# One decoder block on one core: places freed by the products themselves, the first head routed alone, the second tile's attention pairs at slots 8 to 24

## The chip, the core and the metric

The kernel runs on one core of one Trainium2 chip. A core has a matrix engine (PE, TensorE), a vector engine (DVE, VectorE), a scalar engine (ACT, ScalarE), GpSimd (POOL) and a queue engine (SP, SyncE), which run apart from each other and meet at semaphores; 16 DMA engines move data between device memory and the on-chip memory. The metric is the device time of one execution in microseconds (us). The kernel before takes 834.14 us, the median of three runs (832.98 to 834.54).

## The reference, cut to what matters

256 tokens of width 1024 go through one block: a modulation computed from a vector `c`, attention of 16 heads (8 with one causal block, 8 dilated, which on 256 tokens are masks over the same scores), an output projection, a layer norm, and a feed-forward part that picks experts for each token.

```python
mod = silu(c) @ w_ada + b_ada                       # 1024 x 6144
sh1, sc1, g1, sh2, sc2, g2 = split(mod, 6)
h = x * (1 + sc1) + sh1
proj = h @ w_in                                     # 1024 x 3072: q, k, v of both groups
y = rms_norm(attention(proj)) @ w_out
x = layer_norm(ALPHA * x + (1 + g1) * y)
h2 = x * (1 + sc2) + sh2
q = h2 @ w_q                                        # 8 heads of 128
s1, s2 = q[:, :, :64] @ keys0.T, q[:, :, 64:] @ keys1.T      # 128 scores each
e, g = top 16 of the 16 x 16 sums of the top 16 of s1 and of s2, and their softmax
a = gelu(h2 . u[e]) * g                             # 8 x 16 experts for each token
out = layer_norm(ALPHA * x + (1 + g2) * sum(a * v[e]))
```

Each of the 256 tokens reads 128 experts, each a row of 2048 floats (u and v, 8 KB): 268 MB in all.

## The kernel before, in words

**Tiles.** Tokens are two tiles of 128. The gather part has 256 *slots*, 128 to a tile and 16 to a head. A slot is one expert for each of 128 tokens: one indirect DMA by POOL (L1065) brings 1 MB into one *place* of `ring`. DVE takes the dot product of h2 with the row's first half (`dot`, L814); ACT makes gelu, weight and a diagonal matrix of weights (`weigh`, L647 to L660); PE multiplies that matrix by the row's second half and adds it up in two banks (`slot`, L465). Three slots of each 16 between 16 and 111 (`BY_DVE`) are added by DVE instead (`add_slot`, L825 to L828). A gather may start when the slot before it in its place is done.

**Places.** The ring has eight places of 8 KB per partition. Before the gathers they hold the chunks of the weights, so they come free late: 4 and 5 after product `v 1 1`, 6 and 7 after `q 0 1`, 0 and 1 after `v 0 1`, 2 and 3 after the second tile's output products `wo 1 g 0`. Gathers 0 to 35 (`WIDE_FROM`) go round six places (`NARROW`), the later ones round all eight. That a pair is free is told by ACT: a step `free` in its stream waits for the product and counts up `ring_free` (L748), on which POOL waits.

**Order.** One list, `PLAN`, names all steps, and every engine walks through it and does its own part of each step, so the list sets the order on every engine. `gather_steps(i)` gives the steps at slot i: its dot, pieces of the routing of a later head (`piece`, 12 to a head, L845 to L888), what `BESIDE` lists for i, and the products of slot i - 2. `BESIDE` holds the second tile's attention: `S` (scores), `Tr` (transposes), `PV` (values) for pairs of units, then `wo`, `xa`, `ln1a`, `ln1b` (output product, residual, norm) and the queries `q` and scores `s` of the other heads.

**The steps named below.** `wsum c` is the product of silu(c) with column chunk c of `w_ada` on DVE: 8 instructions of 128x512 (L924 or L928, then L937). For chunk 2, terms 3, 6 and 7 are made by PE (`modk`, L521). `modp` and `modc` are column sums on PE (L475) that give shift and scale; `modrow` and `madd` spread the other chunks over the partitions. `qkz`, `qkh`, `qk` are the query and key products (L525, L490), split by halves of the weights. The bias row of the attention is made by PE (`bias`, L533) in bank 0 and read by DVE (L895). A 1 is added to three rows of `mod` by POOL (L1055, L1056). Chunk 11 is loaded as four *patches* into parts of other tiles, since no place is free. `q 0 0` makes the queries of heads 0 and 1 for the first tile, `s 0 0 z` their scores; the routing of head 0 follows, and its end lets the first gather start.

**Banks.** The steps that fill a bank take banks 0 to 5 in turn; two steps (`LATE`) have banks 6 and 7.

## Time and profile before

| | before |
|---|---|
| median of three runs | 834.14 us (832.98 to 834.54) |
| profiled execution, its time and its span | 833.26 us, 831.4 us |
| PE, DVE, ACT, POOL busy | 687.7, 586.9, 340.1, 306.2 us |
| DMA | 323.72 MB, 389 GB/s over the span; 78.2% of the span in the gathers' queue |
| chain that ended last | DMA 52%, PE 29%, DVE 8%, ACT 4% |

The profile is of one execution; its first instruction starts at 0 and its last ends at 831.4 us, so about 1.9 us of that execution's time lie around the span. Busy time is by engine and may overlap. A view of a line, an engine or a stretch gives start and length of instructions, how long the engine was idle before, and what released it; an instruction of PE on 32-bit floats shows as two rows' worth of passes, so 16 products count as x32. The DMA share in a stretch tells how full the 16 DMA engines were, and GB/s what they moved.

### The profile page before, as it was taken

Reading aid. Unit: us, or ns where it says so; the run is one execution under the profiler, and the core shown is the slowest. Engines: PE = TensorE matmul, PEld = TensorE weight load, DVE = VectorE, ACT = ScalarE, POOL = GpSimd, SP = SyncE. Lnnn points to the kernel's source line nnn. Section 1 sums busy time; section 2 is a strip of 40 time slices with the busy share of each in tenths; the row PEclk is TensorE's granted clock in tenths of the full one; section 3 lists DMA queues with packets and bytes.
Section 4 is the critical chain, followed back from the end, with each engine's and each line's share of the span. In section 5 each row is a group of like instructions: output and inputs, shape, how many; then the busy total and the mean of one; then the engine's idle time right before and its main releaser. Section 6 shows DMA issues by size and latency. Waiting matters only on the chain.

```text
span 831.4 us, 7233 instructions
## 1 busy us (share of the span) xinstructions
PE 687.7 (83%) x2000; PEld 330.8 (40%) x2000; DVE 586.9 (71%) x1296; ACT 340.1 (41%) x988; POOL 306.2 (37%) x263
## 2 busy tenths in 40 slices
PE   6999999799998878786979877777778687878874
PEld 3887745545434444442423323222223232222221
DVE  6645886689689767787777777767576757675545
ACT  0012142376636343434454536344443434343333
POOL 5000000234356535554535444543443434434320
PEclk9999999999999998998898999999999999999998
DMA  9999992399999999999999999999999999999991
GB/s 353 401 419 419 376 388 82 149 401 392 375 394 396 421 421 421 421 421 422 421 422 421 421 421 421 423 421 420 421 422 421 422 422 423 420 421 423 420 422 75
DMA packets 48043, 323.72 MB, mean 389 GB/s; under 512 B 5698, under 2 KB 8066, under 8 KB 9346
## 3 DMA queue, kind: packets, MB, share of 16 engines
q0 software_dynamic: 36864, 268.45, 78.2%
q1 hardware_dynamic: 10258, 54.55, 16.5%
q10 hardware_dynamic: 882, 0.27, 0.1%
q8 instruction: 16, 0.26, 0.1%
...
HBM read 322.18 MB, written 1.07 MB: 389 GB/s over the span
## 4 chain that ended last, share of the span: by engine, by line
DMA 52%; PE 29%; DVE 8%; ACT 4%; issue 4%; POOL 2%; SPq 0%; DVEq 0%; ACTq 0%
DMA ring<-in_experts,e_all 50%; PE bank L465 14%; PE bank L490 6%; PE bank L456 4%; DVE ring L814 3%; DVE acc L937 2%; POOL ring L1065 2%; ACT diag L660 1%; DMA lnw<-in_w 1%; PE bank L560 1%; PE bank L579 1%; ACT weight L651 1%; DMA ring<-in_w 1%; ACT gel L647 1%; PE bank L521 1%
## 5 line engine op out<-in xcount | busy, mean ns | idle before, releaser
L465 PE MATMUL bank<-ring,diag 128*128 128x512 f32 x952 | 472.3, 632 | 113.4 <-ACT diag L660 112.8
L1065 POOL DMA_INDIRECT ring<-in_experts,e_all x256 | 293.8, 1148 | 490.7 <-PE bank L465 293.4
L465 PEld LDWEIGHTS bank<-ring,diag 128*128 128x128 f32 x952 | 172.8, 196 | 391.5 <-ACT diag L660 236.8
L814 DVE CUSTOM_DVE_ANT_0 ring<-ring,T_h 128x1024 f32<-128x1024 f32 x128 | 156.8, 1226 | 113.0 <-DMA ring<-in_experts,e_all 113.0
L814 DVE CUSTOM_DVE_ANT_0 ring<-ring,h 128x1024 f32<-128x1024 f32 x128 | 156.7, 1224 | 74.0 <-DMA ring<-in_experts,e_all 72.6
L647 ACT ACTIVATE gel<-pre 128x1 f32<-128x1 f32 x256 | 51.9, 203 | 332.4 <-DVE pre L814 331.5
L660 ACT ACTIVATE diag<-consts,weight 128x128 f32<-128x128 f32 x238 | 95.5, 401 | 7.8
L651 ACT ACTIVATE weight<-gel,g_all 128x1 f32<-128x1 f32 x256 | 75.4, 295 | 9.3
L937 DVE SCALAR_TENSOR_TENSOR acc<-ring,cact,acc 128x512 f32<-128x512 f32 x60 | 49.0, 817 | 2.8
L456 PE MATMUL bank<-ring,hT_yT 128*128 128x512 f32 x80 | 35.5, 594 | 0.0
L490 PE MATMUL bank<-hT_yT,lnw 128*128 128x256 f32 x128 | 30.8, 402 | 1.1 <-DVE hT_yT L907 1.1
L668 ACT COPY QT_h2T<-bank 128x512 f32<-128x512 f32 x6 | 3.5, 580 | 61.0 <-PE bank L490 61.0
L490 PEld LDWEIGHTS bank<-hT_yT,lnw 128*128 128x128 f32 x128 | 25.9, 204 | 5.5 <-issue 1.6
L647 ACT ACT_TABLE_LOAD x21 | 26.9, 1283 | 0.4
L456 PEld LDWEIGHTS bank<-ring,hT_yT 128*128 128x128 f32 x80 | 15.0, 190 | 18.3 <-issue 18.2
L828 DVE SCALAR_TENSOR_TENSOR hT_yT<-ring,weight,hT_yT 128x1024 f32<-128x1024 f32 x17 | 21.8, 1281 | 0.0
L814 DVE DVE_READ_ACCUMULATOR2_ANT pre<- 128x1 f32 x256 | 21.1, 83 | 0.0
L641 ACT ACT_TABLE_LOAD x15 | 19.2, 1283 | 0.3
L701 ACT ACTIVATE probs<-probs,negmax 128x128 f32<-128x128 f32 (+1 forms) x32 | 14.2, 443 | 11.0 <-DVE negmax L957 11.0
L954 DVE SCALAR_TENSOR_TENSOR probs<-bank,T_h 128x512 f32<-128x512 f32 x12 | 8.2, 682 | 10.1 <-PE bank L560 10.1
L579 PE MATMUL bank<-V_x,probs 128*128 128x64 f32 x96 | 11.7, 274 | 4.2 <-issue 4.2
L579 PEld LDWEIGHTS bank<-V_x,probs 128*128 128x128 f32 x96 | 11.6, 192 | 7.4 <-issue 7.4
...
## 6 DMA issues: line engine op xcount, KB each, us to landing
ring<-in_w SPq DMA_DIRECT2D x28, 1024.0 KB, 12.9
H_s<-in_w SPq DMA_DIRECT2D x7, 1024.0 KB, 13.8
lnw<-in_w SPq DMA_DIRECT2D x6, 1024.0 KB, 15.6
ring<-in_experts,e_all POOLq DMA_INDIRECT x256
...
xT_y<-in_xT SPq DMA_DIRECT2D x1, 1024.0 KB, 13.8
x<-in_x SPq DMA_DIRECT2D x1, 1024.0 KB, 16.9
...
```

What stands on the lines that cost most here:

```text
L456: last = nc.tensor.matmul(dst, lhs(k), rhs(k), start=(k == 0), stop=(k == n - 1))
L465: last = nc.tensor.matmul(tile_sum(t)[n], diag[:, m % DIAGS, :], ring[:, RING_AT[i], D + CH * n:D + CH * n + CH], start=(s == 0), stop=(s ...
L490: last = nc.tensor.matmul(dst[:, T * j:T * j + T], w[:, k, P * (2 * i + j):P * (2 * i + j) + P], hT[:, k, :], start=(k == 0 and c >= 2), s ...
L579: last = nc.tensor.matmul(dst[:, HD * j:HD * j + HD], probT[:, step[1] % 2, at:at + P], V_x1[:, kt, c:c + HD], start=(kt == 0), stop=(kt = ...
L641: nc.scalar.activation(bexp[:], bdiff[:], ACT.Exp, accum_out=bsum[:, 0:1]).then_inc(bexp_ready, 1)
L647: own.then(nc.scalar.activation(gel[:, r:r + 1], pre[:, r:r + 1], ACT.Gelu))
L651: ins = nc.scalar.mul(weight[:, r:r + 1], gel[:, r:r + 1], g_all[:, i:i + 1])
L660: nc.scalar.mul(diag[:, m % DIAGS, :], ident, weight[:, r:r + 1]).then_inc(diag_ready, 1)
L814: nc.vector.tensor_tensor_reduce(ring[:, r, 0:D], ring[:, r, 0:D], h2[i // SLOTS], 1.0, 0.0, ALU.mult, ALU.add, pre[:, i % PAIR:i % PAIR + ...
L828: ins = nc.vector.scalar_tensor_tensor(dve_sum, values, weight[:, r:r + 1], dve_sum, ALU.mult, ALU.add)
L937: ins = nc.vector.scalar_tensor_tensor(part, row, cact[:, k:k + 1], part, ALU.mult, ALU.add)
L1065: nc.gpsimd.indirect_dma_start(ring[:, r, :], None, A["experts"], bass.IndirectOffsetOnAxis(ap=e_all[:, i:i + 1], axis=0)).then_inc(slot_i ...
```

## The change

1. `free` and `ring_free` go. POOL waits itself for the bank of the product that empties a pair of places.
2. Of head 0, queries and scores are made alone (`q1 0`, `s1 0 z`), then those of head 1; `q` starts on half of the transposed tile.
3. `wsum 11` moves on DVE from after `wsum 10` to after `ln1b 0`. Its patches change (one of them in `diag`), and the second output chunk is loaded ahead of them on SP. `wsum 7` goes ahead of `yT 0 0`.
4. POOL's additions of 1 go; ACT adds it as the bias of its copy (`madd`).
5. In the opening, `bias` and `modc 0` get banks 6 and 7, term 6 of chunk 2 goes from PE to DVE, and PE has four more products whose result isn't used (`warm`).
6. The second tile's pairs go from slots 0 to 19 to slots 5 to 24, and what follows them from 20 to 32 to 25 to 45. `WIDE_FROM` goes from 36 to 44. A fourth slot in each 16 is added by DVE.
7. ACT loads the table of gelu after `v 0 1` is issued (`gelu`), and copies `v 0 1` at slot 1.
8. Each residual takes its two halves one after the other, and the last slot of a tile signals its first half (`half_done`).

```diff
-BY_PE = {2: (3, 6, 7)}
+BY_PE = {2: (3, 7)}
-WIDE_FROM = 36
+WIDE_FROM = 44
-       ("v", 1, 1), ("free", 0), ("ln1b", 0), ("hT", 0, 0), ("hT", 0, 1), ("S", 4), ("q", 0, 0),
-       ("s", 0, 0, 0), ("s", 0, 0, 1), ("Tr", 4), ("modrow", 7)]
+     ("v", 1, 1), ("ln1b", 0), ("wsum", 11), ("hT", 0, 0), ("hT", 0, 1), ("S", 4), ("q1", 0), ("s1", 0, 0), ("s1", 0, 1), ("q1", 1), ("Tr", 4), ("modrow", 7)]
-BY_DVE = [i for i in range(16, 112) if i % 16 in (2, 4, 5)]
+BY_DVE = [i for i in range(16, 112) if i % 16 in (2, 4, 5, 12)]
...
+APART = [("bias",), ("modc", 0)] + [("wo", 0, 1, n) for n in range(2)]
...
             load(("ada", 10))
+            filled(sp, ("qk", 3, 1))
+            load(("out", 1))
             summed(sp, 9)
...
-            filled(sp, ("qk", 3, 1))
-            load(("out", 1))
...
+                    if s == SLOTS - 1 and n == 0:
+                        last.then_inc(half_done, 1)
...
+                if kind == "warm":
+                    w = places[W_PLACES[CHUNK[("ada", 0)]]]
+                    arrived(pe, CHUNK[("ada", 0)], 0)
+                    for _ in range(step[1]):
+                        nc.tensor.matmul(bank[STEP_BANKS - 1][:, 0:T], ones[:], w[:, 0, 0:T], start=True, stop=True)
...
+                elif kind == "q1":
+                    h = step[1]
+                    w = query_weights(pe, 0, 0)
...
+                    product(dst[:, 0:P], lambda k: w(k)[:, P * h:P * h + P], tokens).then_inc(full, 1)
+                elif kind == "s1":
+                    h, z = step[1:]
+                    pe.wait_ge(gnsk_in, 32)
+                    settle_bank(pe, ("q1", h))
+                    r = slice(HD * z, HD * z + HD)
+                    nc.tensor.matmul(dst[:, 0:NK], query_T(0, 0)[r, h, :], skT[r, :], start=True, stop=True).then_inc(full, 1)
...
+                        nc.scalar.activation(part, src[:], ACT.Identity, bias=ones[:, 0:1]).then_inc(freed(("modrow", m)), 1)
...
+                elif kind == "s1":
+                    act.wait_ge(patch_read, 1)
+                    evacuate(step, scores[:, 0, step[1], step[2], :], filled(act, step)[:, 0:NK])
...
-                for n in range(2):
-                    dve.wait_ge(*f[n][2])
+                    dve.wait_ge(*taken)
...
-            pool.wait_ge(rows_in, 16)
-            nc.gpsimd.tensor_scalar(mod[0:1, G1, :], mod[0:1, G1, :], 1.0, None, ALU.add)
-            nc.gpsimd.tensor_scalar(mod[0:1, SC2:G2 + 1, :], mod[0:1, SC2:G2 + 1, :], 1.0, None, ALU.add).then_inc(rows_one, 1)
+            empty = {4: [("v", 1, 1)], 6: [("q", 0, 1)], 0: [("v", 0, 1)], 2: [("wo", 1, g, 0) for g in range(2)]}
...
-                    pool.wait_ge(ring_free, 1 + sum(before is None for before in RING_BEFORE[:i]))
+                    for step in empty[r // 2 * 2]:
+                        filled(pool, step)
```

The order on PE at the very start, before; the one-column products of `bank<-cact,ring` are `modk`, those of `bank<-ones,acc` are `modp` and `modc`, and the last row is `qkh`:

```order
L525 MATMUL bank<-acc 128x512 x3
L533 MATMUL bank<-probs,relT 16x384
L525 MATMUL bank<-acc 128x512
L513 MATMUL bank<-acc 128x16
L475 MATMUL bank<-ones,acc 128x1 x4
L521 MATMUL bank<-cact,ring 128x1 x12
L475 MATMUL bank<-ones,acc 128x1 x4
L490 MATMUL bank<-hT_yT,lnw 128x256 x16
```

And now; the rows `bank<-ring,ones` are `warm`:

```order
L535 MATMUL bank<-acc 128x512 x3
L543 MATMUL bank<-probs,relT 16x384
L535 MATMUL bank<-acc 128x512
L519 MATMUL bank<-acc 128x16
L524 MATMUL bank<-ring,ones 128x256 x2
L531 MATMUL bank<-cact,ring 128x1 x4
L480 MATMUL bank<-ones,acc 128x1 x4
L524 MATMUL bank<-ring,ones 128x256
L531 MATMUL bank<-cact,ring 128x1 x4
L524 MATMUL bank<-ring,ones 128x256
L480 MATMUL bank<-ones,acc 128x1 x4
L495 MATMUL bank<-hT_yT,lnw 128x256 x16
```

The bias row and the shift have other banks, four of the twelve `modk` rows are gone, and the column sums of chunk 0 come after the first `modk`.

The order on DVE from the norm of the first tile (its last instruction is `h_0<-h_0,lnst,mod`) to the start of head 0's routing (`MAX`), before; `probs` is pair 4 of the attention:

```order
L797 SCALAR_TENSOR_TENSOR h_0<-x,lnst,mod 128x1024
L802 RECIPROCAL lnst<-lnst 128x1
L808 SCALAR_TENSOR_TENSOR h_0<-h_0,lnst,mod 128x1024
L954 SCALAR_TENSOR_TENSOR probs<-bank,T_h 128x512
L957 TENSOR_REDUCE negmax<-probs 128x2
L845 MAX v<-H_s 128x8 x2
```

And now, where the rows with `cact` are `wsum 11`:

```order
L825 SCALAR_TENSOR_TENSOR h_0<-x,lnst,mod 128x1024
L830 RECIPROCAL lnst<-lnst 128x1
L836 SCALAR_TENSOR_TENSOR h_0<-h_0,lnst,mod 128x1024
L956 SCALAR_TENSOR_TENSOR acc<-H_s,cact,mod 128x512
L967 SCALAR_TENSOR_TENSOR acc<-H_s,cact,acc 128x512 x3
L967 SCALAR_TENSOR_TENSOR acc<-xT_y,cact,acc 128x512 x2
L967 SCALAR_TENSOR_TENSOR acc<-V_x,cact,acc 128x512
L967 SCALAR_TENSOR_TENSOR acc<-diag,cact,acc 128x512
L984 SCALAR_TENSOR_TENSOR probs<-bank,T_h 128x512
L987 TENSOR_REDUCE negmax<-probs 128x2
L873 MAX v<-H_s 128x8 x2
```

Eight instructions stand now ahead of pair 4 and of the routing.

The order on PE from the transposes of the first tile to the product `v 0 1` (`bank<-ring,hT_yT`), before; `bank<-xT_y,ring` are queries, `bank<-skT,acc` their scores:

```order
L599 MATMUL bank<-consts,h_0 128x128 x8
L560 MATMUL bank<-KT_qT,QT_h2T 128x256 x2
L456 MATMUL bank<-xT_y,ring 128x128 x16
L616 MATMUL bank<-skT,acc 128x128 x4
L567 MATMUL bank<-consts,probs 128x128 x4
L550 MATMUL bank<-acc,ones 128x512
L456 MATMUL bank<-xT_y,ring 128x128 x16
L616 MATMUL bank<-skT,acc 128x128 x4
L560 MATMUL bank<-KT_qT,QT_h2T 128x256 x2
L579 MATMUL bank<-V_x,probs 128x64 x4
L456 MATMUL bank<-ring,hT_yT 128x512 x8
```

And now:

```order
L609 MATMUL bank<-consts,h_0 128x128 x8
L570 MATMUL bank<-KT_qT,QT_h2T 128x256 x2
L459 MATMUL bank<-xT_y,ring 128x128 x8
L639 MATMUL bank<-skT,acc 128x128 x2
L459 MATMUL bank<-xT_y,ring 128x128 x8
L577 MATMUL bank<-consts,probs 128x128 x4
L560 MATMUL bank<-acc,ones 128x512
L639 MATMUL bank<-skT,acc 128x128 x2
L459 MATMUL bank<-xT_y,ring 128x128 x16
L646 MATMUL bank<-skT,acc 128x128 x4
L570 MATMUL bank<-KT_qT,QT_h2T 128x256 x2
L589 MATMUL bank<-V_x,probs 128x64 x4
L459 MATMUL bank<-ring,hT_yT 128x512 x8
```

Eight products of queries instead of sixteen stand ahead of the first scores.

## Rows read from the trace of the kernel before

**Rows 1.** the page's second part: GB/s moved by the DMA engines in 40 slices.

```profile
GB/s 353 401 419 419 376 388 82 149 401 392 375 394 396 421 421 421 421 421 422 421 422 421 421 421 421 423 421 420 421 422 421 422 422 423 420 421 423 420 422 75
```

**Rows 2.** windows: busy time and count per engine, granted PE clock, DMA share, GB/s.

```profile
140.00:156.00 16.00, 13.74 (x109) 11.87 (x107) 9.41 (x35) 7.13 (x18) 0.00 (x0) 1.00 0.00 1
156.00:168.00 12.00, 8.85 (x31) 4.77 (x31) 6.17 (x21) 5.23 (x13) 5.85 (x6) 0.98 0.82 319
168.00:200.00 32.00, 29.60 (x101) 15.05 (x100) 28.20 (x78) 23.36 (x60) 11.13 (x10) 0.95 1.00 400
200.00:260.00 60.00, 56.34 (x186) 28.57 (x184) 49.53 (x118) 33.76 (x89) 31.72 (x23) 1.00 0.98 380
360.00:800.00 440.00, 352.66 (x762) 131.49 (x760) 304.59 (x709) 193.18 (x581) 192.59 (x177) 0.97 1.01 421
```

**Rows 3.** timeline: start, length, instruction, count, [idle before]. POOL, then DVE.

```profile
13.99 5.68 POOL L1056 TENSOR_SCALAR mod<-mod 1x2048 f32<-1x2048 f32 x1
...
14.48 4.01 DVE L937 SCALAR_TENSOR_TENSOR acc<-ring,cact,acc 128x512 f32<-128x512 f32 x1
```

**Rows 4.** timeline of PE, 18 to 52 us.

```profile
18.14 5.26 PE L521 MATMUL bank<-cact,ring 128*128 128x1 f32 x24
...
26.17 9.56 PE L490 MATMUL bank<-hT_yT,lnw 128*128 128x256 f32 x32 [1.07 <-DVE hT_yT L907]
...
36.38 3.70 PE L490 MATMUL bank<-hT_yT,H_s 128*128 128x256 f32 x16
...
44.27 7.07 PE L490 MATMUL bank<-hT_yT,lnw 128*128 128x256 f32 x32
```

**Rows 5.** timeline of SP: the load of an input chunk's first half is issued.

```profile
6.91 0.79 SPq L369 DMA_DIRECT2D H_s<-in_w  x1
```

**Rows 6.** DMA issues in 6.91 to 6.93 us: us from issue to landing.

```profile
H_s<-in_w SPq DMA_DIRECT2D x1, 1024.0 KB, 25.7
```

**Rows 7.** timeline of PE, 120 to 141 us.

```profile
120.76 3.67 PE L456 MATMUL bank<-lnw,h 128*128 128x512 f32 x8 [1.58 <-DMA lnw<-in_w]
...
139.62 1.04 PE L599 MATMUL bank<-consts,h 128*128 128x128 f32 x8
```

**Rows 8.** timeline of DVE, 109 to 149 us.

```profile
109.24 5.54 DVE L937 SCALAR_TENSOR_TENSOR acc<-ring,cact,acc 128x512 f32<-128x512 f32 x7
...
137.10 1.29 DVE L808 SCALAR_TENSOR_TENSOR h<-h,lnst,mod 128x1024 f32<-128x1024 f32 x1
141.82 0.69 DVE L954 SCALAR_TENSOR_TENSOR probs<-bank,T_h 128x512 f32<-128x512 f32 x1 [3.44 <-PE bank L560]
...
147.53 0.49 DVE L845 MAX8 v<-H_s 128x8 f32<-128x128 f32 x2 [4.30 <-ACT H_s L668]
```

**Rows 9.** timeline of ACT, 143 us: the first exponential of pair 4.

```profile
143.27 0.51 ACT L701 ACTIVATE probs<-probs,negmax 128x256 f32<-128x256 f32 x1 [0.52 <-DVE negmax L957]
```

**Rows 10.** timeline of POOL: gathers 0, 6 and 26 are issued.

```profile
156.20 1.15 POOL L1065 DMA_INDIRECT ring<-in_experts,e_all  x1 [136.53 <-DVE e_all L883]
...
171.49 0.94 POOL L1065 DMA_INDIRECT ring<-in_experts,e_all  x1 [5.82 <-PE bank L465]
...
230.65 1.83 POOL L1065 DMA_INDIRECT ring<-in_experts,e_all  x1 [6.82 <-DVE hT_yT L828]
```

**Rows 11.** the page's fifth part: groups by line; count, then busy us, mean ns.

```profile
L814 DVE CUSTOM_DVE_ANT_0 ring<-ring,h 128x1024 f32<-128x1024 f32 x128 | 156.7, 1224 | 74.0 <-DMA ring<-in_experts,e_all 72.6
...
L828 DVE SCALAR_TENSOR_TENSOR hT_yT<-ring,weight,hT_yT 128x1024 f32<-128x1024 f32 x17 | 21.8, 1281 | 0.0
```

**Rows 12.** windows, 168 to 172 us.

```profile
168.00:172.00 4.00, 4.00 (x8) 1.45 (x8) 3.96 (x13) 1.33 (x5) 0.51 (x1) 0.62 1.01 426
```

**Rows 13.** timeline of PE, 166 to 168 us.

```profile
166.68 1.09 PE L579 MATMUL bank<-V_x,probs 128*128 128x64 f32 x8 [3.15 <-issue]
```

**Rows 14.** timeline, the last slot's products on PE and what DVE does next.

```profile
820.79 1.98 PE L465 MATMUL bank<-ring,diag 128*128 128x512 f32 x4 [0.49 <-ACT diag L660]
...
822.91 1.29 DVE L776 TENSOR_TENSOR acc<-bank,mod 128x512 f32<-128x512 f32 x2 [3.17 <-PE bank L465]
```

More of the change, by code:

```diff
@@ L149 @@
 STEP_BANKS = 6
-NO_FILL = ("qkz", "qkh", "modp", "modk", "ny", "xa", "rows2", "ln1a", "ln1b", "x1", "piece", "madd", "wsum", "free", "dot", "slot", "fold", "ln2a", "ln2b", "ln2c")
+NO_FILL = ("qkz", "qkh", "modz", "modp", "modk", "warm", "vcopy", "gelu", "ny", "xa", "rows2", "ln1a", "ln1b", "x1", "piece", "madd", "wsum", "dot", "slot", "fold", "ln2a", "ln2b", "ln2c")
 FILLS = [s for s in PLAN if s[0] not in NO_FILL]
-LATE = [("wo", 0, 1, n) for n in range(2)]
-PLACE = {s: (n % STEP_BANKS, n // STEP_BANKS) for n, s in enumerate(s for s in FILLS if s not in LATE)}
-PLACE |= {s: (STEP_BANKS + n % 2, n // 2) for n, s in enumerate(LATE)}
+APART = [("bias",), ("modc", 0)] + [("wo", 0, 1, n) for n in range(2)]
+PLACE = {s: (n % STEP_BANKS, n // STEP_BANKS) for n, s in enumerate(s for s in FILLS if s not in APART)}
+PLACE |= {s: (STEP_BANKS + n % 2, n // 2) for n, s in enumerate(APART)}
 RING_AT = [(NARROW[i % len(NARROW)] if i < WIDE_FROM else WIDE[(i - WIDE_FROM) % RING]) for i in range(NT * SLOTS)]
@@ L502, in _ @@
                     if i == 0:
-                        for late in LATE:
-                            settle_bank(pe, late)
+                        for step_apart in APART:
+                            settle_bank(pe, step_apart)
                     if i == SLOTS:
@@ L737, in _ @@
                     route_exp(step[1])
-                elif kind == "free":
-                    if step[1] == 0:
-                        filled(act, ("v", 1, 1))
-                        act.sem_inc(ring_free, 2)
-                    elif step[1] == 1:
-                        filled(act, ("q", 0, 1))
-                        act.sem_inc(ring_free, 2)
-                    elif step[1] == 2:
-                        filled(act, ("v", 0, 1))
-                        act.sem_inc(ring_free, 2)
-                    else:
-                        for g in range(2):
-                            filled(act, ("wo", 1, g, 0))
-                        act.sem_inc(ring_free, 2)
+                elif kind == "gelu":
+                    own.settle()
+                    own.then(nc.scalar.activation(spare[:], epsc[:], ACT.Gelu))
                 elif kind == "dot":
@@ L841, in route @@
                     dve.wait_ge(consts_in, 32)
-                    for z in range(2):
-                        settle_bank(dve, ("s", t, h // 2, z))
+                    for scored in [("s1", head, z) if head < 2 else ("s", t, h // 2, z) for z in range(2)]:
+                        settle_bank(dve, scored)
                     for z in range(2):
@@ L935, in _ @@
                         own.settle()
[L936 removed]
+                        if patched and patch_of[k] == (1, 0):
+                            dve.sem_inc(patch_read, 1)
+                        row = patches[patch_of[k][0]][:, patch_of[k][1], :] if patched else w[:, k, :]
                         ins = nc.vector.scalar_tensor_tensor(part, row, cact[:, k:k + 1], part, ALU.mult, ALU.add)
```

93 lines of the change are left out of this document (53 added, 40 removed), and 20 rows, old and new, of tables (BESIDE, PLAN).

## The prediction, made before the changed kernel ran

> **What bounds the kernel now.** I read the page's strip of DMA rates first [rows 1]. It says that the chip's memory is busy nearly all the time: about 420 GB/s in the slices in which the weights come, a hole in slices 7 and 8, then a ragged stretch of 375 to 401, and from slice 14 on a flat 421. So the kernel is a stream of weights, a hole, and a stream of gathers. Windows over the stages put numbers on it [rows 2]. From 360 to 800 us nothing but the gathers counts: 177 of them in 440 us are 2.49 us each at 421 GB/s, while PE is busy 80% and DVE 69%. No edit of PE, DVE or ACT work is worth anything there. In the hole, 140 to 156 us, the DMA share is 0.00: the gathers wait for the first head's routing. From 156 to 260 us the gathers run, but below 421.
>
> The time is therefore: start of gather 0, plus a fixed stream, plus what the stream loses at its beginning, plus a tail. Against 421 GB/s the windows lose 12 x (1 - 319/421) = 2.9 us, 32 x (1 - 400/421) = 1.6 and 60 x (1 - 380/421) = 5.8, in all 10.3. About 1.9 of the first is the way from the issue of gather 0 to its first bytes, which stays; 8.4 us could be won in the ramp. The other two terms are the start, at 156.20 [rows 10], and the tail.
>
> **The opening.** PE's wait on the chain ends with the shift and scale at 25 us. Three edits touch it. First, POOL's additions. One DVE instruction that ran beside POOL's 5.68 us took 4.01 us [rows 3], against 0.79 for one of seven in a row (5.54/7) [rows 8]: 3.2 us. Second, 8 of the 24 passes of `modk` leave PE, 5.26/3 = 1.75 us [rows 4], and one term of 0.79 is added on DVE, which has just been given 3.2. Third, PE doesn't wait for the bias row any more. Against this stand four `warm` products of 256 columns; 32 passes of that width took 9.56 us early and 7.07 later [rows 4], so eight passes are 2.4 us at the early price, and they fill waits for the weights of chunk 2. Sum: DVE ends chunk 2 about 3 us earlier, PE gets there about as early, and the first product of `qkh` starts some 4 us before 26.17.
>
> I don't book 4. The product `qkh 1 0` needs its weights, issued at 6.91 and landed 25.7 later, at 32.6 [rows 5, 6]. It starts at 36.38 now [rows 4]. The loads are all issued in one go and stream at full rate, so 32.6 stays, and the gain there is 36.38 - 32.6 = 3.8 at most. From there PE goes from product to product; I take 3.7. Ends: 2.2 if PE, having waited for the weights, comes back at its half clock; 3.8.
>
> That half clock is seen once near here: after 3.15 us of idleness [rows 13] the granted clock of 168 to 172 us is 0.62 [rows 12], that is, mostly the lower level (1.2 instead of 2.4 GHz), and 4 x 0.38 = 1.5 us of full-speed work is lost. The wait in the changed opening would be some 2.5 us.
>
> The Trainium skill (TensorE: Matmul & The Clock Gate, HAM oscillation) says that an array left waiting for DMA falls back to half its clock and starts its next work cold. Rows 12 and 13 agree with that. By the rule the opening brings 2.2 and not 3.7, and the time is 1.5 later than I say. The same skill (SBUF — State Buffer, Who interferes with whom) says that a DVE instruction with two on-chip inputs and a POOL instruction that reads there exclude each other for the whole instruction. The trace shows the loss, but 4.01 us is less than POOL's 5.68; by the rule in full the additions held up to 5.7 - 0.8 = 4.9 instead of 3.2. That changes nothing here, since 32.6 is the limit either way.
>
> **Up to the first scores.** PE waits 1.58 us at 120.76 for the second output chunk [rows 7], which is loaded behind the patches; loaded ahead of them it comes about 5 us sooner. Gain 1.6 (ends 0 and 1.6). Then the moved `wsum 11`. Now it is eight instructions in front of work that waits for PE; moved, it stands behind `ln1b 0` and before pair 4. The norm ends at 137.10 + 1.29 = 138.4 [rows 8]; with 5.3 gained, at 133.1. Eight instructions at 0.79 take it to 139.4. Pair 4 follows (0.69 and a maximum of the same length [rows 8]), to 140.9. Who is queued behind? ACT: its exponentials of pair 4 come before its copy of the first queries, and they wait for that maximum [rows 9]. They end 1.1 later, at 142.0. PE's eight products of queries are ready at about 138.3, so here the shorter first query brings nothing: the copy waits for ACT. Copy, two scores, two copies: 143.5 against 147.53 [rows 8]. The start of the routing moves by 4.0 and not 5.3. The cover of `wsum 11`, DVE's 3.44 us of idleness before pair 4, is too small for its 6.3 us. Ends: 2.5 (if the opening gives 2.2) and 5.3.
>
> The routing is the same instructions, 147.53 to 156.20. So gather 0 goes at 152.2: **4.0 us**.
>
> **The ramp.** Now gather 6, the first to reuse a place, is issued 15.3 us after gather 0 [rows 10], and gathers 6 to 26 take 230.65 - 171.49 = 59.2 us, 2.96 each. From 168 to 260 us PE is busy 85.9 of 92 us and DVE 77.7 [rows 2]: PE, which has three pairs' attention and the slots to do, is what keeps places from coming free. Changed: pairs 6 to 11 start at slot 8, so the first slots meet an idle PE, no value product stands before slot 0, ACT has gelu's table loaded, and its copy of `v 0 1` is out of the way. Gather 6 goes then about 11 us after gather 0, before the DMA engines have finished the first six (15 us). The same work is spread over 24 slots (60 us of stream) instead of 20 (50).
>
> Who is late next is DVE. Slots 8 to 23 want 16 dots at 1.31 (1.22 and the read), 21 us; a head's routing, 8.7; three pairs of scores at 2.8, 8.3; three slots at 1.28 [rows 11], 3.8; some 3 of smaller steps. That is 45 us against 16 x 2.49 = 40. Slots 24 to 47 add the residual and the norm, about 9, and the twelfth slot of a turn (1.28 each): DVE ends some 5 to 6 us behind the stream. Six places are 14.9 us of stream; dot, weight, products and issue take some 5 of them and the way of a gather 4 to 5, so about 4 to 5 can be behind. DVE will make the stream wait a little. I keep about 3.9 of the 8.4 as lost and book **4.5**. Ends: 0 and 8.4.
>
> Removing ACT from the release of the places is part of this; by itself it is half a microsecond once.
>
> **The tail.** The last slot's products take 1.98 from 820.79, DVE starts at 822.91 [rows 14]. With half a slot signalled, its first product starts 1.0 earlier; but gate and sum now alternate and each waits for the other, so it ends **0.6** earlier (ends 0 and 1.0).
>
> Sum: 4.0 + 4.5 + 0.6 = 9.1 us. The profiled execution took 833.26, so 824.2; the median is 0.9 higher, so **825** by it.
>
> **Rivals.**
>
> *Only the start and the tail are won.* DVE falls back as far as the ramp's slack, and the stream loses the same 8.4. For it: DVE is busy 77.7 of 92 us now, and nothing is taken from it. Against: PE is busier. 834.1 - 4.6 = 829.5.
>
> *The whole ramp is won.* If six places hold the DVE's lag, all 8.4 come: 834.1 - 13.0 = 821.
>
> *It does not do what it says at the start.* The weights stream without a gap up to 104 us, so if later chunks, too, are what PE waits for, and ACT holds the queries as worked out, the start moves by 1 or less, and with the ramp as it is the time is 833.5. Against: PE waits for weights once after 27 us, the 1.58.
>
> *Slower: the narrow ring.* Gathers up to 43 instead of 35 go round six places. If the places come free as slowly as between gathers 6 and 26, every 2.96 us, for 18 more gathers, 18 x 0.47 = 8.5 us are lost, of which the trace loses some 1.5 there already; less 4.6 that is 2.4 slower: 836.5. It decides once DVE is more than about 10 us behind at slot 44. Against: PE's share of the delay is what the edit removes.
>
> *The half clock*, by the page's rule above, would give 826.5; it lies inside the forecast's own range.
>
> **How the numbers follow.** Forecast 0.50, with a range of its own from 823 to 828; start and tail only 0.20; whole ramp 0.17; no effect 0.07; slower 0.06. The range from 820.5 to 831 leaves out the last two and the far end of the third. What a measurement here can tell from none is 0.2%, 1.7 us: faster 0.87 (the first three), same 0.07, slower 0.06.
>
> **What would show it.** In the changed profile: no DVE instruction of the opening over 1 us; the second group of `qkh` near 32.6, after a wait for DMA; no wait for DMA at the output products; ACT idle before pair 4's exponential, and its copy of the first queries right behind; the first gather near 152; gather 6 about 11 us later; 395 to 410 GB/s in the 100 us after. I am wrong if gather 0 goes after 155, if the ramp loses more than 8 us, or if anything changes in the 421 GB/s of the long stretch.

## The result and the profile after

The changed kernel takes 846.83 us (median of 4 runs, 846.63 to 847.71) against 834.34 (median of 4 runs, 832.98 to 839.32): ratio 1.0138, 95% interval 1.0113 to 1.0163. It is **slower** by 12.5 us. Forecast was 825, so not even the sign was right. The profiled execution has a span of 844.9 us, 13.5 more than before.

The strip of DMA rates of the profile's page, as in [rows 1], and the shares of the chain that ended last:

```profile
GB/s 356 398 421 419 423 334 50 202 372 369 327 394 358 347 364 422 421 421 422 422 421 421 422 420 421 407 425 420 422 422 422 420 421 422 421 421 422 421 422 92
DMA 45%; PE 36%; DVE 7%; issue 5%; ACT 5%; POOL 2%; DVEq 0%; ACTq 0%
```

The hole at slices 7 and 8 is there as before. Behind it stood five slices of 375 to 401, and 421 GB/s from slice 14 on; now there are seven of 327 to 394, and the full rate begins at slice 16. In the chain PE went from 29% to 36% and DMA from 52% to 45%: the products carry what the stream carried. Windows of the changed kernel, as in [rows 2], with two more (the one of 280 to 300 us lies in the one above it):

```profile
140.00:156.00 16.00, 11.22 (x70) 9.79 (x70) 10.01 (x37) 4.60 (x17) 2.12 (x3) 0.79 0.06 11
156.00:168.00 12.00, 11.78 (x31) 5.87 (x32) 8.54 (x26) 5.31 (x16) 2.50 (x3) 0.86 0.83 336
168.00:200.00 32.00, 27.01 (x86) 13.98 (x84) 21.42 (x59) 17.33 (x46) 12.21 (x12) 0.89 0.93 366
200.00:260.00 60.00, 51.83 (x182) 29.39 (x183) 45.68 (x112) 35.23 (x94) 22.96 (x20) 0.89 0.95 360
260.00:300.00 40.00, 32.28 (x76) 13.55 (x74) 34.82 (x76) 18.63 (x49) 17.03 (x14) 0.96 0.89 332
280.00:300.00 20.00, 13.34 (x32) 5.41 (x30) 18.37 (x47) 10.27 (x26) 9.84 (x7) 0.91 0.81 300
360.00:800.00 440.00, 353.45 (x789) 135.60 (x788) 311.18 (x716) 191.88 (x579) 195.75 (x175) 0.95 1.01 421
```

The long stretch is untouched (421 both times). Against 421 the ramp loses 12 x (1 - 336/421) = 2.4 us, 32 x (1 - 366/421) = 4.2, 60 x (1 - 360/421) = 8.7 and 40 x (1 - 332/421) = 8.5: 23.8 us, where the kernel before lost 10.3 and had reached full rate at 260. The deepest hole behind the start is 280 to 300 us, with 300 GB/s; there DVE is busy 18.37 of 20 us and PE 13.34. The granted clock fell too: 0.79 in 140 to 156 us, 0.89 in 200 to 260, where it was 1.00 both times.

The timeline of PE answers to [rows 4, 7]: the opening, the second output chunk, the transposes, and then the wait for the first scores.

```profile
22.71 10.19 PE L495 MATMUL bank<-hT_yT,lnw 128*128 128x256 f32 x32 [1.08 <-DVE hT_yT L935]
...
33.54 3.70 PE L495 MATMUL bank<-hT_yT,H_s 128*128 128x256 f32 x16
...
41.42 7.07 PE L495 MATMUL bank<-hT_yT,lnw 128*128 128x256 f32 x32
...
116.18 3.65 PE L459 MATMUL bank<-lnw,h 128*128 128x512 f32 x8
...
135.02 1.04 PE L609 MATMUL bank<-consts,h 128*128 128x128 f32 x8
...
143.19 0.89 PE L639 MATMUL bank<-skT,acc 64*128 64x128 f32 x4 [4.10 <-ACT acc L698]
144.01 3.78 PE L459 MATMUL bank<-xT_y,ring 128*128 128x128 f32 x16
...
156.22 1.13 PE L570 MATMUL bank<-KT_qT,QT_h2T 64*128 64x256 f32 x4 [1.25 <-ACT mod L718]
...
158.22 8.78 PE L459 MATMUL bank<-ring,hT_yT 128*128 128x512 f32 x16
```

The transposes start at 135.02 instead of 139.62. Then the 4.10 us of waiting for ACT begin, the second head's query products take 3.78 us for sixteen (2.05 in run c3 below, at a granted clock of 1.00), `S 5` waits 1.25 us for its bank, and `v 0 1` takes 8.78 instead of 7.09 (before, from 156.00). DVE, as in [rows 8], and POOL, as in [rows 10], of the same kernel; the POOL rows are gathers 0, 4, 6, 26, 42 and 43:

```profile
13.41 3.97 DVE L967 SCALAR_TENSOR_TENSOR acc<-ring,cact,acc 128x512 f32<-128x512 f32 x5
...
144.61 0.49 DVE L873 MAX8 v<-H_s 128x8 f32<-128x128 f32 x2 [2.84 <-ACT H_s L698]
```

```profile
153.27 1.08 POOL L1091 DMA_INDIRECT ring<-in_experts,e_all  x1 [149.03 <-DVE e_all L911]
...
167.27 0.94 POOL L1091 DMA_INDIRECT ring<-in_experts,e_all  x1 [9.19 <-PE bank L459]
169.75 0.94 POOL L1091 DMA_INDIRECT ring<-in_experts,e_all  x1 [0.30 <-issue]
...
232.48 1.71 POOL L1091 DMA_INDIRECT ring<-in_experts,e_all  x1 [1.80 <-DVE hT_yT L856]
...
279.95 1.78 POOL L1091 DMA_INDIRECT ring<-in_experts,e_all  x1 [3.20 <-DVE hT_yT L856]
285.44 1.68 POOL L1091 DMA_INDIRECT ring<-in_experts,e_all  x1 [3.71 <-DVE hT_yT L856]
```

Gather 0 leaves 2.9 us earlier than before. Gather 4 leaves 14.0 us after it, and the advance is gone. In the kernel before it left 7.3 us after it:

```profile
163.49 0.94 POOL L1065 DMA_INDIRECT ring<-in_experts,e_all  x1 [2.40 <-ACTq L748]
```

Later gathers tell where the time goes. Against the kernel before, gather 26 leaves 1.8 us later (232.48 for 230.65), gather 35 leaves 7.6 us later (259.87 for 252.30) and gather 43 leaves 15.2 us later (285.44 for 270.22). Gathers 42 and 43 wait for DVE's additions of slots 36 and 37. The one of slot 37 starts at 283.90, behind the dot of slot 39 and `ln1a` (280.85 to 283.90), which the new table puts at slot 39.

The tail, as in [rows 14]; DVE now takes the first half of the sum while PE is still at the second:

```profile
834.87 1.98 PE L468 MATMUL bank<-ring,diag 128*128 128x512 f32 x4 [0.47 <-ACT diag L690]
```

```profile
836.13 0.69 DVE L804 TENSOR_TENSOR acc<-bank,mod 128x512 f32<-128x512 f32 x1 [2.31 <-PE bank L468]
```

The ledger of the 13.5 us: start -2.9, gather 0 to the last dot +17.0 (its dot starts at 832.6 instead of 818.5), tail -0.6.

### The profile page after: what moved, and what is told of

It is laid out like the page before. It is cut to its first block, busy times and chain, and to the rows that moved or that the text cites. A ratio compares the mean times of both kernels' runs of the same rounds, so it can differ in the third digit from the quotient of the medians.

```text
span 844.9 us, 7203 instructions
## 1 busy us (share of the span) xinstructions
PE 696.5 (82%) x1976; PEld 335.7 (40%) x1976; DVE 592.5 (70%) x1303; ACT 341.1 (40%) x988; POOL 295.0 (35%) x261
## 4 chain that ended last, share of the span: by engine, by line
DMA 45%; PE 36%; DVE 7%; issue 5%; ACT 5%; POOL 2%; DVEq 0%; ACTq 0%
DMA ring<-in_experts,e_all 44%; PE bank L468 16%; PE bank L495 7%; PE bank L459 6%; DVE ring L842 3%; POOL ring L1091 2%; PE bank L589 1%; ACT diag L690 1%; PE bank L570 1%; ACT weight L681 1%; PE bank L560 1%; DMA probs<-in_maskrow 1%; ACT gel L677 1%; ACT junk L705 1%; DVE hT_yT L856 1%
## 5 line engine op out<-in xcount | busy, mean ns | idle before, releaser
L468 PEld LDWEIGHTS bank<-ring,diag 128*128 128x128 f32 x928 | 170.3, 199 | 394.5 <-ACT diag L690 239.8
L690 ACT ACTIVATE diag<-consts,weight 128x128 f32<-128x128 f32 x232 | 93.1, 401 | 7.6
L967 DVE SCALAR_TENSOR_TENSOR acc<-ring,cact,acc 128x512 f32<-128x512 f32 x61 | 45.9, 752 | 2.8
L459 PE MATMUL bank<-ring,hT_yT 128*128 128x512 f32 x80 | 37.2, 618 | 0.0
L856 DVE SCALAR_TENSOR_TENSOR hT_yT<-ring,weight,hT_yT 128x1024 f32<-128x1024 f32 x23 | 29.4, 1277 | 0.0
L589 PE MATMUL bank<-V_x,probs 128*128 128x64 f32 x96 | 14.3, 311 | 9.5 <-issue 9.5
L589 PEld LDWEIGHTS bank<-V_x,probs 128*128 128x128 f32 x96 | 13.9, 226 | 13.0 <-issue 13.0
```

What stands on the lines that cost most here:

```text
L459: last = nc.tensor.matmul(dst, lhs(k), rhs(k), start=(k == 0), stop=(k == n - 1))
L468: last = nc.tensor.matmul(tile_sum(t)[n], diag[:, m % DIAGS, :], ring[:, RING_AT[i], D + CH * n:D + CH * n + CH], start=(s == 0), stop=(s ...
L589: last = nc.tensor.matmul(dst[:, HD * j:HD * j + HD], probT[:, step[1] % 2, at:at + P], V_x1[:, kt, c:c + HD], start=(kt == 0), stop=(kt = ...
L690: nc.scalar.mul(diag[:, m % DIAGS, :], ident, weight[:, r:r + 1]).then_inc(diag_ready, 1)
L856: ins = nc.vector.scalar_tensor_tensor(dve_sum, values, weight[:, r:r + 1], dve_sum, ALU.mult, ALU.add)
L967: ins = nc.vector.scalar_tensor_tensor(part, row, cact[:, k:k + 1], part, ALU.mult, ALU.add)
```

## The experiments

All times are medians, each beside the kernel before on the same chip (835.06 to 835.67 us for the experiments). A difference in us is against that; between two experiments it is the difference of these differences, or of the times as given. An interval of 0.3% to either side is 2.5 us, so differences of 2 us or less between two experiments are uncertain.

| run | us | ratio to before, interval |
|---|---|---|
| changed | 846.83 | 1.0138 [1.0113, 1.0163] |
| a1 old gather schedule in the changed kernel | 831.25 | 0.9961 [0.9945, 0.9977] |
| a2 changed, three DVE slots | 846.44 | 1.0145 [1.0123, 1.0168] |
| b1 before, new schedule | 846.62 | 1.0142 [1.0117, 1.0166] |
| b2 before, four DVE slots | 837.33 | 1.0035 [1.0012, 1.0058] |
| c1 before, joining at 44 | 839.81 | 1.0044 [1.0024, 1.0065] |
| f2 before, joining at 40 | 836.99 | 1.0033 [1.0001, 1.0066] |
| e1 f2 and followers late | 840.63 | 1.0060 [1.0035, 1.0084] |
| e2 e1 and last pair late | 840.61 | 1.0061 [1.0036, 1.0086] |
| c2 e2 and other pairs late | 844.44 | 1.0126 [1.0080, 1.0172] |
| f1 e1, DVE slots along | 838.78 | 1.0046 [1.0029, 1.0063] |
| d1 c2, DVE slots along | 841.07 | 1.0058 [1.0029, 1.0087] |
| d4 changed, DVE slots moved | 846.15 | 1.0127 [1.0090, 1.0164] |
| c3 a1, wsum 11 early | 831.91 | 0.9946 [0.9924, 0.9967] |
| c4 c3, row 7 early | 828.71 | 0.9919 [0.9891, 0.9948] |
| e3 c4 once more | 829.12 | 0.9926 [0.9897, 0.9954] |
| e4 a1, row 7 early | 828.99 | 0.9920 [0.9890, 0.9950] |
| c5 c4, `v 0 1` first | 832.93 | 0.9974 [0.9953, 0.9996] |
| d3 c4, joining at 34 | 831.36 | 0.9959 [0.9932, 0.9986] |

### Is it the order of the gather stage?

Theory S: the table `BESIDE` and the later `WIDE_FROM` make the kernel slower and the other edits faster. Rivals: L (the late gather 4 and the half clock at the start), D (the fourth slot in sixteen that DVE adds).

**a1**, the changed kernel with the old table, `WIDE_FROM = 36` and three DVE slots:

```
-WIDE_FROM = 44
+WIDE_FROM = 36
-BY_DVE = [... if i % 16 in (2, 4, 5, 12)]      BESIDE as before
+BY_DVE = [... if i % 16 in (2, 4, 5)]
```

> The changed kernel with the gather part's three tables of the kernel before: pairs at slots 0 to 19, six places up to gather 35, three slots of sixteen on DVE. Theory S (the schedule of the first 44 slots costs what was lost): start 3 us and tail 0.6 us earlier are left and the ramp loses about what it lost before, 829 to 832. Rival L (the late product v 0 1, with PE at its half clock, upsets the ramp by itself): 836 to 843.

**a2**, the changed kernel with `(2, 4, 5)` alone:

> The changed kernel with three instead of four slots of sixteen on DVE. Theory D (the fourth slot overloads DVE and leaves PE idle, so that its clock falls): 836 to 842. Theory S with the pairs and the six places as cause: 845 to 848, no change from the changed kernel. Rival L: no change either.

**b1**, the kernel before with the new table and `WIDE_FROM = 44` alone:

> The kernel before, with only the second tile's pairs and what follows them at their new slots and six places up to gather 43. Theory S: 842 to 850, the whole loss and no gain. Theory D: 836 or less. Rival L: within 2 us of before.

**b2**, the kernel before with `(2, 4, 5, 12)` alone:

> The kernel before with only the fourth slot of sixteen on DVE. Theory D: 838 to 842. Theories S and L: within 2 us of before, since the long stretch waits for DMA.

Measured: 831.25, 846.44, 846.62 and 837.33. The two schedule edits carry the whole loss by themselves (+11.6 in the kernel before), and without them the change is a gain of 3.8 us. That gain belongs to all the other edits together; apart from the place of `wsum 11` (below) none of them was run alone. The fourth DVE slot costs 2.3 us in the kernel before, a little more than the 2 that S and L allowed, and nothing measurable beside the new schedule. Theory S holds; D falls. L is not the loss, but what it names is real (below).

### The narrow ring

**c1** and **f2**, the kernel before with one number changed:

```
-WIDE_FROM = 36
+WIDE_FROM = 44      (c1)
+WIDE_FROM = 40      (f2)
```

> The kernel before with its own slots for the pairs, and places 2 and 3 joining the ring at gather 44 in place of 36; all else as before. b1 (pairs at 8 to 24 and six places to gather 43 together) lost 11.6 us. Theory R (the shorter ring carries it): each of gathers 36 to 43 then waits for the dot and the product six slots earlier, eight slots at about 1 us: 841 to 847 us. Theory P (the place of the pairs at slots 8 to 24 carries it: while gathers are young, a late Tr copy on ACT holds back a weight, and TensorE idles and is then at .50): 835 to 838 us, since in the trace of b1 the stream is already 7 to 8 us behind before slot 36.

> The kernel before with places 2 and 3 joining at gather 40 in place of 36; nothing else. Joining at 44 cost 3.7 us (c1). Theory B: 0 to 2 us more than before (half of it): 835.5 to 837.5. Rival H: 3 us or more.

Measured: +4.1 us for eight gathers and +1.7 for four (an interval that begins at 0.01%). The expectation of R for c1 (841 and more) and that of P (838 and less) both missed: the ring is a third of the loss. The windows say where. First the kernel before, then c1:

```profile
260.00:280.00 20.00, 14.85 (x40) 6.76 (x40) 17.24 (x35) 9.27 (x31) 12.30 (x10) 0.91 1.01 423
280.00:300.00 20.00, 17.98 (x68) 9.52 (x68) 12.91 (x35) 7.86 (x26) 7.80 (x7) 1.00 1.02 422
```

```profile
260.00:280.00 20.00, 13.52 (x57) 7.56 (x56) 15.34 (x30) 10.40 (x31) 7.74 (x7) 0.94 0.97 387
280.00:300.00 20.00, 18.87 (x65) 10.03 (x66) 14.65 (x38) 7.74 (x25) 8.66 (x7) 0.89 0.99 379
```

387 and 379 GB/s instead of 423 and 422: 40 x (1 - 383/421) = 3.6 us, right where gathers 36 to 43 are issued (264.34 to 283.68). No engine is full in these rows: PE and DVE are less busy than before in the first window and more in the second, 18.87 for 17.98 and 14.65 for 12.91. What the edit changed is that the places are fewer.

### The pairs and their followers

**c2** is the kernel before with pairs 5 to 11 at the new slots, the followers packed behind them and joining at 40. **e1** has only the followers late, **e2** the followers and the last pair.

```
     all three: 25: ny, 26: yT, 27/29/31/33: wo, 30: xa, 34: free and ln1a,
                36: ln1b, 37: q 0 2, 39/40: s 0 2, 42/43: hT 1, 46: q 0 3
-    19: [("PV", 10), ("PV", 11)], 22: [("wo", 1, 1, 1)] ...        (before)
+    19: [("PV", 10), ("PV", 11)], 27: [("wo", 1, 1, 1)] ...        (e1)
+    24: [("PV", 10), ("PV", 11)], others as before                 (e2)
+    5: Tr 5, 7: PV 5, 8: S 6 ... 18: PV 8, 24: PV 10               (c2)
```

> The kernel before with the second tile's pairs at slots 8 to 24, the followers packed behind them (ny 25, yT 26, wo 27 to 33, ln1a 34, ln1b 36, queries of heads 4 and 5 at 37, hT 42) and places 2 and 3 joining at gather 40, when the last wo product is done; all else as before. Theory P: 841 to 847 us, low GB/s between 200 and 300 us as in b1. Theory R: 835 to 838 us, since the ring is six places wide for only four gathers more than before.

> The kernel before with all pairs at their own slots 3 to 19, but the followers at the slots of c2 (ny 25, wo 27 to 33, ln1a 34, queries of heads 4 and 5 at 37, hT 42) and places 2 and 3 joining at gather 40, as in c2 (+8.8 us). Theory K (the last pair, at 20 to 24, meets the third head's routing and the slots that DVE adds; TensorE idles and falls to half clock): at most 3 us slower than before, 836 to 839 us. Rival F (the followers carry it: four wo products of 3.60 us then stand where every slot is TensorE's, and TensorE is full from 242 to 275 us in c2): 840 to 844 us.

> e1 with the last pair, heads' units 10 and 11, at slots 20, 22 and 24 as in c2; units 5 to 9 stay at 0 to 13. Theory K: 3 to 6 us more than e1, and the clock of 220:240 falls as in c2 (0.80). Rival F: within 1.5 us of e1.

Measured, against before: e1 +5.2, e2 +5.2, c2 +8.8. So the followers carry 5.2 us, of which the later joining is 1.7; the last pair carries nothing that can be measured, and the earlier pairs 3.6. Theory K falls, and with it my reading of the half clock. The windows 220:240 of e1, then e2, then c2 (the last but two numbers are the granted clock):

```profile
220.00:240.00 20.00, 11.40 (x33) 5.68 (x32) 12.83 (x27) 5.90 (x20) 9.27 (x7) 0.75 0.96 371
```

```profile
220.00:240.00 20.00, 14.59 (x46) 8.69 (x45) 15.88 (x36) 14.91 (x38) 8.19 (x7) 0.74 0.93 373
```

```profile
220.00:240.00 20.00, 16.64 (x52) 9.31 (x52) 14.79 (x31) 10.38 (x29) 9.24 (x7) 0.80 0.86 323
```

All three fall to 0.74 to 0.80, e1 without a late pair. So low a clock comes with a loss of 5.2 us as well as with one of 8.8; here it doesn't set the time.

What the followers do is seen in the timeline of PE. First the kernel before, where `wo 1 1 1` and `wo 1 1 0` follow each other, because slots 20 and 21 are added by DVE:

```profile
221.78 3.60 PE L456 MATMUL bank<-lnw,hT_yT 128*128 128x512 f32 x8
225.21 3.60 PE L456 MATMUL bank<-ring,hT_yT 128*128 128x512 f32 x8
230.23 1.98 PE L465 MATMUL bank<-ring,diag 128*128 128x512 f32 x4 [1.43 <-ACT diag L660]
```

Then e1:

```profile
234.94 6.26 PE L465 MATMUL bank<-ring,diag 128*128 128x512 f32 x8 [8.60 <-ACT diag L660]
...
243.20 3.60 PE L456 MATMUL bank<-lnw,hT_yT 128*128 128x512 f32 x8
246.63 3.60 PE L465 MATMUL bank<-ring,diag 128*128 128x512 f32 x8
250.07 3.60 PE L456 MATMUL bank<-ring,hT_yT 128*128 128x512 f32 x8
253.50 3.60 PE L465 MATMUL bank<-ring,diag 128*128 128x512 f32 x8
```

In e1 PE is idle for 8.60 us. Slots 20 and 21 are DVE's, so PE's next work is slot 22, and its dot starts only at 232.66, after 3.76 us of waiting for the gather. Afterwards PE has all four products to do, and is busy without a gap from 243.20 to 277.8 us: three times a product of 3.60 us is followed by the eight matmuls of two slots, 6.87 us for two gathers, which the stream could bring in 2 x 2.49. In the kernel before the first two of the four run in the time that PE has to spare (it still waits 1.43 us for ACT behind them).

**f1** and **d1** test this: e1 and c2 with the first three DVE slots moved by the same five slots; **d4** does it in the changed kernel.

```
-BY_DVE = [i for i in range(16, 112) if i % 16 in (2, 4, 5)]
+BY_DVE = [i for i in range(16, 112) if (i % 16 in (2, 4, 5) and i > 21) or i in (23, 25, 26)]
```

> e1 (all pairs at their own slots, followers at 25 to 43, joining at gather 40; 840.63 us, +5.2) with the first three slots that DVE adds moved by the same five, from 18, 20 and 21 to 23, 25 and 26. Theory B (in the kernel before the first two wo products of 3.60 us run while DVE adds slots 20 and 21 and TensorE has no slot of its own; in e1 all four alternate with two slots each, 6.87 us for two gathers that need 5.0, from 243 to 272 us): 836.5 to 838.5 us, and the window 260:280 rises from 325 to over 390 GB/s. Rival H (the ring that joins at 40 instead of 36, or the queries' later place, carries it): 840 to 841.5 us.

> c2 (the kernel before with the pairs at 8 to 24, +8.8 us) with the first three slots that DVE adds moved along with the pairs, from 18, 20 and 21 to 23, 25 and 26; later DVE slots as before. In the trace of c2 TensorE stands idle for 2.49, 2.66 and 0.69 us between 213 and 231 us, because slots 18, 20 and 21, which DVE adds, lie among the last two pairs and leave TensorE only four matmuls a slot for the others, and then is full from 242 to 275 us, where four wo products of 3.60 us meet slots that all are TensorE's. Theory M (the meeting of the pairs and of the wo products with the DVE slots carries P): the clock in 220:240 comes back from 0.80 to over 0.95, the windows 220:240 and 260:280 rise from 323 and 328 to over 370 GB/s, and the time is 837 to 841 us. Rival Q (the ring's six places are what a pair needs early; DVE slots are indifferent): 843 to 846 us, the windows as in c2.

> The changed kernel with its DVE slots 18, 20 and 21 moved to 23, 25 and 26; all else as changed (846.83 us). Theory M: the half clock in 220:240 and part of the holes at 200:240 and 260:300 go, 840 to 844 us. Rival Q: 846 to 848 us.

Measured: f1 838.78 (1.8 less than e1), d1 841.07 (3.4 less than c2), d4 846.15 (no change). By a hair f1 and d1 miss the ranges of B (to 838.5) and M (to 841). Windows of e1 and then of f1:

```profile
260.00:280.00 20.00, 17.84 (x66) 9.59 (x64) 16.21 (x32) 11.93 (x27) 8.61 (x7) 1.00 0.91 325
```

```profile
260.00:280.00 20.00, 16.08 (x62) 8.99 (x61) 18.38 (x32) 10.72 (x29) 6.40 (x6) 0.81 0.96 389
```

The window 260:280 rises from 325 to 389 GB/s, where theory B asked for over 390, and the rates of 240:260 fall meanwhile from 383 to 365. In d1 the clock of 220:240 is back at 1.00, as M said, and 260:280 rises from 328 to 404 GB/s, but 220:240 only from 323 to 335. Both kernels are faster, though their intervals overlap those of their partners, so the sign of the 1.8 and the 3.4 is likely and their size is not known. The miss of d4 fits: in the changed kernel the `wo` products stand at 31 to 38, where slots 23 to 26 relieve nothing. That is argued from the table; a version with DVE slots at 29 to 32 was not tried. And beside the last two products there DVE has slots 34, 36 and 37 already: from 254.18 to 278.5 us PE does four `wo` products and the six slots that it has of 29 to 37, which is 2.7 us for each of the nine, and not the 3.43 of e1. So e1 shows how the followers can hold PE up; it doesn't show what held up the changed kernel, whose deepest hole comes later, at 280 to 300 us, with DVE late.

### The new wait at the start

a1 has the 4.10 us wait, the half clock, and gather 4 at 166.95, 14.0 us after gather 0. Theory W: these hold back some of the gain of the opening. All runs of this part start from a1. **c3** puts the last weighted sum back to its old place, **c4** also copies `modrow 7` ahead of the routing, **e4** does only the latter, **e3** is c4 once more:

```
-     ("v", 1, 1), ("ln1b", 0), ("wsum", 11), ("hT", 0, 0) ...      (c3, c4)
+     ("wo", 0, 0, 0), ("wsum", 11), ("PV", 2) ...
-     ("Tr", 4), ("modrow", 7)] + [... pieces ...] + [("madd", 7), ("S", 5)
+     ("Tr", 4), ("modrow", 7), ("madd", 7)] + [... pieces ...] + [("S", 5)     (c4, e4)
```

> a1 (the changed kernel with the slots, the ring and the three DVE slots of before, 831.25 us) with the last weighted sum back behind the first wo product, as in the kernel before. Theory W (the 4.10 us for which TensorE waits for ACT at 142.91, and its half clock until 164 us, push the values product of the second tile and with it gathers 4 and 5 to 167 us): the wait goes, TensorE stays at 1.00, gather 4 is issued near 163 us, and the time is 827 to 829 us. Rival V (DVE sets the start: the last sum ahead of ln1 delays the routing by its 3 us again): routing and gather 0 are 2.5 to 3 us later, and the time is 832 to 835 us.

> c3 with the copy of modrow 7 ahead of the first head's routing on ACT instead of behind it, so that S 5 does not wait 1.25 us for its bank. Theory W: another 0.5 to 1.5 us less than c3, gather 4 earlier by 1.25 us. Rival (gather 4 is not what the ramp waits for): the same as c3 within 1 us.

> c4 again, unchanged, beside the others on one chip: 828.71 us before, ratio 0.9919. If the margin is real: ratio 0.990 to 0.995. If c4 only met a good chip or few runs: 0.996 to 0.998, as a1, c5 and d3.

> a1 with the copy of modrow 7 ahead of the first head's routing on ACT, the last weighted sum left behind ln1 as in the changed kernel. The 4.10 us wait of TensorE stays, so by theory W its clock is at half until 156 us or later; S 5 no longer waits 1.25 us. If both edits of c4 are needed to keep the clock: gather 4 near 165 us and 830 to 832 us. If the wait for the bank alone put the half clock into the values product: that product takes 7.1 us again, and 828 to 829.5 us.

Measured: c3 831.91, c4 828.71, e3 829.12, e4 828.99. c3 misses W's 827 to 829, and V's 832 to 835: the wait of 4.10 us shrinks to 0.95 and PE keeps its clock to 154 us, but then `S 5` waits for its bank all the same, and `v 0 1` is slow. First c3, PE from `S 5` to `v 0 1`; then e4, from the first head's scores on:

```profile
154.20 1.13 PE L570 MATMUL bank<-KT_qT,QT_h2T 64*128 64x256 f32 x4 [1.26 <-ACT mod L718]
155.26 1.10 PE L589 MATMUL bank<-V_x,probs 128*128 128x64 f32 x8
156.20 8.78 PE L459 MATMUL bank<-ring,hT_yT 128*128 128x512 f32 x16
```

```profile
142.39 0.85 PE L639 MATMUL bank<-skT,acc 64*128 64x128 f32 x4 [4.10 <-ACT acc L698]
143.17 3.37 PE L459 MATMUL bank<-xT_y,ring 128*128 128x128 f32 x16
...
154.06 1.10 PE L589 MATMUL bank<-V_x,probs 128*128 128x64 f32 x8
155.00 7.09 PE L459 MATMUL bank<-ring,hT_yT 128*128 128x512 f32 x16
```

And e4's gathers 0 and 4:

```profile
152.38 1.08 POOL L1091 DMA_INDIRECT ring<-in_experts,e_all  x1 [148.13 <-DVE e_all L911]
...
162.35 0.94 POOL L1091 DMA_INDIRECT ring<-in_experts,e_all  x1 [5.17 <-PE bank L459]
```

e4 keeps the 4.10 us wait and its half clock (3.37 us for sixteen products), but the clock is back by `v 0 1`: 7.09 us, and gather 4 leaves 10.0 us after gather 0. It is as fast as c4. So the wait for the bank was the costly one; the 4.10 us wait, much longer, cost nothing that can be measured, and the place of `wsum 11` doesn't matter either. Moving one step in the order of the program is worth 2.3 us on top of a1 (828.99 against 831.25, on two chips) and 3.2 on top of c3 (828.71 against 831.91, on one). In each comparison the intervals overlap a little, but both, and e3, say the same; c4 missed W's 0.5 to 1.5 us less than c3 to the good side. And e4 beats both kernels: 6.4 us less than the kernel before.

Two attempts to go further failed. **c5** puts `v 0 1` ahead of `S 5` and `PV 4`; **d3** lets the two places join at 34.

```
-    [("S", 5), ("PV", 4), ("v", 0, 1), ("gelu",)]
+    [("v", 0, 1), ("S", 5), ("PV", 4), ("gelu",)]      (c5)
-WIDE_FROM = 36
+WIDE_FROM = 34      (d3)
```

> c4 (828.71 us) with the values product of the second tile ahead of S 5 and PV 4, so that gather 4 goes out near 159 us, right behind gather 3, in place of 162.31. Theory G (gather 4 gates the start one to one, as between c3 and c4, where 2.94 us earlier gave 3.2 us): 826 to 827 us. Rival F (four gathers of 1.05 MB fill the DMA engines for some 10 us from gather 0, 153.7 to 164, so gather 4 at 162.3 was just in time): 828 to 830 us, within 1 us of c4.

> c4 with places 2 and 3 joining the ring at gather 34 in place of 36. The mirror of c1, in which joining eight gathers later cost 3.7 us. If the cost is even per gather, this gains 0.9 us (827.8); if the ring is wide enough once the last wo product at slot 28 is done, and gather 34 only waits for that product as it did for slot 28, it is the same as c4 within 0.5 us.

Measured: c5 832.93, d3 831.36. c5 is outside both of its theories. Its gathers 4 and 6:

```profile
161.91 0.94 POOL L1091 DMA_INDIRECT ring<-in_experts,e_all  x1 [2.17 <-PE bank L459]
...
173.44 0.94 POOL L1091 DMA_INDIRECT ring<-in_experts,e_all  x1 [9.35 <-PE bank L468]
```

Gather 4 is early, as meant, but gather 6 leaves 18.5 us after gather 0 (c4: 12.7): the chain `S 5`, `Tr 5`, `PV 5` stands ahead of the first slot's products and begins, counted from gather 0, some 7 us later. d3 is outside both of its expectations, 827.8 and c4's time within 0.5 us. It gained nothing; whether it is really slower than c4 the overlapping intervals leave open.

## Why the prediction was wrong, step by step

- **What bounds the kernel**: right. The long stretch has 421 GB/s in every run; apart from the tail all differences lie before 320 us.
- **POOL's additions** (3.2 us): right. The first term that DVE sums is 5 instructions in 3.97 us now, none of 4.01 is left. PE's first product behind the chain, `qkh 0 0`, starts at 22.71, 3.5 earlier (I said some 4).
- **The limit at 32.6** (gain 3.7): it never bound. The second group starts at 33.54, pushed by PE, which took 10.19 us for the first 32 passes instead of 9.56. The gain is 2.8, between my ends 2.2 and 3.8, though for another reason than theirs.
- **The output chunk** (1.6): the wait is gone, and the term was too small for most executions: it was read from a good one. In c1, whose opening is the kernel's before, the same place reads

```profile
121.32 6.73 PE L456 MATMUL bank<-lnw,h 128*128 128x512 f32 x8 [1.89 <-DMA lnw<-in_w]
```

  where [rows 7] had 3.67 us: a wait of 1.89 us and then half clock. Over the ten profiles with the old opening gather 0 leaves between 155.8 and 159.8 us, median 158.3; over the ten with the new one between 152.0 and 154.9, median 153.2. The change made the opening faster by about 5 us.
- **`wsum 11`** (-1.3): mechanism as told (ACT's exponentials hold the first query's copy), and the start of the routing came at 144.61 for 143.5, gather 0 at 153.27 for 152.2. But c3 shows that the old place gives the same start within 0.3 us, so the move neither costs nor gives.
- **The ramp** (4.5 of gain): this step failed, twice over. (1) I let the first slots find PE idle, and gather 6 leave 11 us after gather 0; it left 16.5 us after. I did not follow the banks of the steps ahead of slot 0 (which step filled a bank last, and which engine empties it). Steps take six banks in turn, and `q1` and `s1` are more steps than `q 0 0` and its scores were. So `S 5`, which used the bank of `s 0 0 1` before, now gets that of `modrow 7`, whose copy stands on ACT behind the routing's exponential. That wait took back some 2.3 us of the opening's gain (e4 against a1; in the changed kernel the same order wasn't run). (2) I spread the work over more slots and summed it per engine over whole stretches, so the schedule counted as a gain. It cost 11.6 us (b1), of which the narrow ring by itself costs 4.1 (c1). The sums missed what meets what. In e1, with the followers alone moved, three `wo` products stand beside slots that PE must add and run PE at 3.43 us a slot (f1 moves the DVE slots and gives back some 1.8). In the changed kernel DVE is late next, as I said, but not "a little": `ln1a` stands ahead of the addition of slot 37, and with six places gathers 42 and 43 wait for DVE's additions of slots 36 and 37, in the window with 300 GB/s; b1 shows the same (gathers 42 and 43 at 280.59 and 285.72, DVE busy 18.45 of 20 us). No run moved `ln1a` alone, so what this place costs is not measured.
- **The tail** (0.6): right, 12.3 us from the last dot to the end instead of 12.9.
- **The rival of the narrow ring**: right in its sign and kind, and given 0.06. It took 8.5 us for 18 gathers at 2.96, less 1.5; measured, the ring costs 4.1 for eight. Alone it would have cancelled the gain of the other edits (3.8). The followers (3.5 beside the joining) and the earlier pairs (3.6) came on top, which no case of mine had. The three add up to 11.2 of b1's 11.6, but two of them were measured beside followers packed at 25 to 43, not at b1's slots.
- **The half clock** rule of the Trainium skill (TensorE: Matmul & The Clock Gate, HAM oscillation), that work behind a wait starts cold, is seen in the traces at once: 3.78 us for sixteen products behind 4.10 us of waiting. But a price could be measured only where PE's next product freed a place.

That b1 and the changed kernel are equal, though the latter's gather 0 leaves 4.5 us earlier (153.27 for 157.77), can be followed in the two traces. The late `v 0 1` puts gather 5 at 168.51 in the changed kernel and at 166.30 in b1, and its dot starts at 176.33 and 176.84: half a microsecond is left of the lead. Gather 11 leaves at 186.38 and 185.90, gather 43 at 285.44 and 285.72.

Not settled: why the pairs 5 to 9 five slots later cost 3.6 us (c2 against e2, whose intervals overlap a little); about 1.7 of the followers' 5.2 (e1 less the joining and less what f1 gives back); and how much of the 11.6 us hangs on DVE at slots 36 to 39.
